# Sample attention with the queries in the partitions: keys and values stream through TensorE, later sums come from a backward scan

## What is computed

```python
def stick_breaking_block(q, k, v, q_pos, k_pos):
    z = jnp.einsum('bthd,bshd->bhts', q, k) * (SB_HEAD_DIM ** -0.5)
    mask = k_pos[None, :] < q_pos[:, None]
    log_fail = jnp.where(mask, jax.nn.log_sigmoid(-z), 0.0)
    after = lax.cumsum(log_fail, axis=3, reverse=True) - log_fail
    a = jnp.where(mask, jnp.exp(jax.nn.log_sigmoid(z) + after), 0.0)
    return jnp.einsum('bhts,bshd->bthd', a, v)
```

## Time and profile before

| | us |
|---|---|
| median of 3 runs | 1241.44 (1239.06 to 1242.43) |
| profiled execution, its time | 1239.74 |
| span of its trace | 1237.9 |
| PE busy | 1185.4 (96% of the span) |
| DVE busy | 743.7 (60%) |
| ACT busy | 461.7 (37%) |
| POOL busy | 293.5 (24%) |
| TensorE clock granted, mean | 0.964 |

### The profile page before, as it was taken

The page is one execution under the profiler, slowest core; times in us unless marked ns, Lnnn a source line. Parts: engine busy times, 40 slices in busy tenths (PEclk is TensorE's granted clock), DMA queues, the critical chain, the costliest instruction groups (busy, mean ns, idle before and its releaser), DMA issues.

```text
span 1237.9 us, 17578 instructions
## 1 busy us (share of the span) xinstructions
PE 1185.4 (96%) x6684; PEld 1122.9 (91%) x6684; DVE 743.7 (60%) x1316; ACT 461.7 (37%) x901; POOL 293.5 (24%) x318
## 2 busy tenths in 40 slices
PE   3999999999999999999999999999999999999994
PEld 2899889999989999988999989899999999998993
DVE  7758955687966588886378885476442133243118
ACT  4356532155542145643034644234402322252221
POOL 2114412113422123423013342120020011111225
PEclk9999988999998899998899998899999999999997
DMA  6130120015031115021014103202310111111144
GB/s 225 35 124 35 35 103 23 32 37 160 18 102 35 37 37 160 18 83 54 20 55 139 39 18 120 75 20 79 124 52 34 52 35 51 35 44 42 35 170 153
DMA packets 41460, 84.92 MB, mean 69 GB/s; under 512 B 2080, under 2 KB 22176, under 8 KB 41248
## 3 DMA queue, kind: packets, MB, share of 16 engines
q1 hardware_dynamic: 40800, 81.43, 19.8%
q10 hardware_dynamic: 576, 2.36, 0.5%
HBM read 67.27 MB, written 16.52 MB: 68 GB/s over the span
## 4 chain that ended last, share of the span: by engine, by line
PE 86%; DVE 9%; issue 2%; ACT 2%; DMA 1%; POOL 1%; SPq 0%; DVEq 0%; POOLq 0%; ACTq 0%
PE bank L619 51%; PE bank L907 7%; PE bank L692 5%; PE bank L732 5%; PE bank L753 3%; PE bank L784 3%; PE bank L830 2%; PE bank L853 2%; PE bank L679 1%; PE bank L678 1%; DVE SPsL L1461 1%; DVE xw L1333 1%; DVE imaskL L1294 1%; POOL SUs L1680 1%; DVE xl L1566 1%
## 5 line engine op out<-in xcount | busy, mean ns | idle before, releaser
L619 PE MATMUL bank<-xl,wh 128*128 128x384 f32 x1344 | 466.2, 347 | 6.7 <-DVE xl L1329 6.7
L619 PE MATMUL bank<-xh,wh 128*128 128x384 f32 x1344 | 464.0, 345 | 6.7 <-ACT xh L1088 3.5
L619 PE MATMUL bank<-xh,wl 128*128 128x384 f32 x1344 | 463.0, 344 | 0.0
L619 PEld LDWEIGHTS bank<-xl,wh 128*128 128x128 f32 x1344 | 260.0, 193 | 14.4 <-DVE xl L1329 8.2
L619 PEld LDWEIGHTS bank<-xh,wh 128*128 128x128 f32 x1344 | 260.4, 194 | 13.0 <-issue 8.4
L619 PEld LDWEIGHTS bank<-xh,wl 128*128 128x128 f32 x1344 | 259.4, 193 | 7.1 <-issue 3.4
L1241 DVE CAST wh<-wr 128x1024 fp32r<-128x1024 f32 x64 | 44.1, 689 | 107.2 <-PE bank L619 107.1
L1694 POOL TENSOR_TENSOR imaskH<-i_nat,k 128x512 fp32r<-128x512 f32 (+1 forms) x36 | 52.1, 1450 | 230.7 <-PE bank L830 230.7
L1032 ACT ACTIVATE slot<-bank,ngate 128x384 f32<-128x384 f32 x48 | 27.7, 578 | 199.1 <-PE bank L619 196.7
L1243 DVE TENSOR_TENSOR wl<-wr,wh 128x1024 fp32r<-128x1024 f32 x64 | 99.1, 1549 | 2.2
L1706 POOL TENSOR_TENSOR slot<-slot,slot 128x384 f32<-128x384 f32 x24 | 31.3, 1303 | 240.6 <-DVE slot L1562 240.6
(11 more groups left out here) (200 smaller groups left out, 1894.5 us busy)
## 6 DMA issues: line engine op xcount, KB each, us to landing
wr<-wch SPq DMA_DIRECT2D x64, 512.0 KB, 3.6
KTc<-ckT SPq DMA_DIRECT2D x4, 2048.0 KB, 9.8
Vc<-cv SPq DMA_DIRECT2D x4, 2048.0 KB, 8.4
xw<-xT SPq DMA_DIRECT2D x6, 768.0 KB, 9.9
graw<-gated SPq DMA_DIRECT2D x8, 576.0 KB, 6.1
xres<-xT SPq DMA_DIRECT2D x1, 4608.0 KB, 15.6
yT<-yb SPq DMA_DIRECT2D x6, 576.0 KB, 3.0
okT<-kT ACTq DMA_DIRECT2D x4, 576.0 KB, 3.0
```

The costliest lines, as they stand in the source:

```text
L619: i = nc.tensor.matmul(CH[n % 2][:, 0:WIN], weights[:, k, :], rows[:, k, w * WIN:(w + 1) * WIN], start=(m == 0), stop=(m == 23))
```

## The change

The sample attention is turned round. The queries become the stationary weights, 32 of them (one stream: 2 heads, 16 tokens), and the 512 cached keys of the stream move: 8 matmuls of 512 columns, each written to 32 partitions of a bank, four streams to a bank. So a query has its scores in one partition, and the later sums are a running sum along the row: DVE scans each row backward over 640 columns (`SW`: 512 cached and 128 new keys) and subtracts the sum from the scores. The splits into high and low, POOL's tile sums and the 18 sum matmuls fall away. For the values the keys must be in the partitions again: PE turns the weights by 10 transposes, ACT copies them to SBUF (`As`), and 32 matmuls take 32 query columns as weights while 128 value columns move. The output has the queries in the partitions; DVE copies it to `Os`, and PE turns it by two transposes in step 3, after which DVE gates it, now in step 3 too. The mask of the new keys is turned once at the start of the kernel. `gg`, `em`, `EK` and `EQ` stand behind the copies of step 1 on ACT, and DVE has its part of the sample attention ahead of the centring of the decays. Steps, pieces and the order of everything else stay.

```diff
+SW = PAST + P
...
-        Es = place("Es", [P, 5, 256])
-        SPs = place("SPs", [P, 5, 256])
-        SUs = place("SUs", [P, 3, 256])
+        Es = place("Es", [P, 2, SW])
+        CUs = place("CUs", [P, 2, SW])
+        As = place("As", [P, 5, 256])
         EK = place("EK", [P, TOK])
         EQ = place("EQ", [P, TOK])
...
+        Os = place("Os", [P, 256])
...
             pe.wait_ge(s_c, 32)
+            for g in range(2):
+                i = nc.tensor.transpose(OB[:, P * g:P * g + P], smask[:, P * g:P * g + P], ident)
+            i.then_inc(s_mt, 1)
             x_square_sum(0)
...
-                        qall = qbd[:, :, :, :].rearrange("p i h t -> p (i h t)")
-                        nc.tensor.matmul(Z[2][:, 0:256], kTs[:, :], qall, start=True, stop=True).then_inc(s_zs, 1)
-                        for half in (1, 0):
-                            for j2 in range(2):
-                                for s in range(STREAMS):
-                                    o = 256 * j2 + 32 * s
-                                    i = nc.tensor.matmul(Z[half][:, o:o + 32], KT_[:, s, P * (2 * half + j2):P * (2 * half + j2 + 1)],
-                                                         qall[:, 32 * s:32 * s + 32], start=(j2 == 0 and s == 0), stop=True,
-                                                         skip_group_check=True)
+                        for g in range(2):
+                            own = qbd[:, 4 * g:4 * g + 4, :, :].rearrange("p i h t -> p (i h t)")
+                            i = nc.tensor.matmul(Z[2][:, P * g:P * g + P], own, kTs[:, :], start=True, stop=True)
+                        i.then_inc(s_zs, 1)
+                        for g in range(2):
+                            for r in range(4):
+                                q = qbd[:, 4 * g + r, :, :].rearrange("p h t -> p (h t)")
+                                i = nc.tensor.matmul(Z[g][32 * r:32 * r + 32, :], q, KT_[:, 4 * g + r, :], start=True, stop=True)
                             i.then_inc(s_zs, 1)
                     if m == 1:
...
-                        for j in (3, 2, 1, 0):
-                            bk = Z[j // 2][:, 256 * (j % 2):256 * (j % 2) + 256]
-                            if j == 2:
-                                pe.wait_ge(s_Shs, p + 1)
-                                pe.wait_ge(s_Sls, p + 1)
...
+                        for g in range(2):
+                            pe.wait_ge(s_asm, 2 * p + g + 1)
+                            for j in range(4):
+                                nc.tensor.transpose(Z[g][:, P * j:P * j + P], Es[:, g, P * j:P * j + P], ident)
+                            nc.tensor.transpose(Z[2][:, P * g:P * g + P], Es[:, g, PAST:SW], ident).then_inc(s_ast, 1)
                     if m == 2:
                         pe.wait_ge(s_gA, 2 * (p + 1))
-                        pe.wait_ge(s_asm, p + 1)
-                        nc.tensor.matmul(OB[:, 0:256], vs[:, :], Es[:, 4, :], start=True, stop=True)
+                        pe.wait_ge(s_ate, p + 1)
+                        for g in range(2):
+                            nc.tensor.matmul(OB[:, P * g:P * g + P], As[:, 4, P * g:P * g + P], vs[:, :], start=(g == 0), stop=True,
+                                             skip_group_check=True)
                         pe.wait_ge(s_kv[1], 16 * (p + 1))
-                        pe.wait_ge(s_as, 3 * (p + 1))
                         for j in (3, 2, 1, 0):
-                            for s in range(STREAMS):
-                                i = nc.tensor.matmul(OB[:, 32 * s:32 * s + 32], V_[:, s, j, :], Es[:, j, 32 * s:32 * s + 32],
-                                                     start=False, stop=True, skip_group_check=True)
+                            for n in range(STREAMS):
+                                g, r = divmod(n, 4)
+                                i = nc.tensor.matmul(OB[32 * r:32 * r + 32, P * g:P * g + P], As[:, j, 32 * n:32 * n + 32],
+                                                     V_[:, n, j, :], start=False, stop=True, skip_group_check=True)
                         i.then_inc(s_os, 1)
+                    if m == 3:
+                        pe.wait_ge(s_oso, p + 1)
+                        for g in range(2):
+                            i = nc.tensor.transpose(OB[:, 2 * P + P * g:2 * P + P * g + P], Os[:, P * g:P * g + P], ident)
+                        i.then_inc(s_ost, 1)
...
+                    if m == 1:
+                        for g in range(2):
+                            act.wait_ge(s_cs, 2 * p + g + 1)
+                            nc.scalar.activation(Es[:, g, :], CUs[:, g, :], ACT.Exp).then_inc(s_as, 1)
+                        for g in range(2):
+                            act.wait_ge(s_ast, 2 * p + g + 1)
+                            nc.scalar.activation(As[:, 0:4, P * g:P * g + P], Z[g][:, :].rearrange("s (j c) -> s j c", j=4), ACT.Copy)
+                        nc.scalar.activation(As[:, 4, :], Z[2][:, 0:256], ACT.Copy).then_inc(s_ate, 1)
 
                         act.wait_ge(s_ge, 2 * (p + 1))
                         nc.scalar.activation(gg[:, :], be[:, :], ACT.Exp).then_inc(s_EX, 1)
...
+                        for g in range(2):
+                            e = Es[:, g, 0:PAST]
+                            dve.wait_ge(s_Ls, 3 * p + g + 2)
+                            V.scalar_tensor_tensor(e, e, 88.0, Z[g][:, :], ALU.min, ALU.max).then_inc(s_sps, 1)
+                            dve.wait_ge(s_sps, 3 * p + g + 2)
+                            dve.wait_ge(s_spm, p + 1)
+                            V.tensor_tensor_scan(CUs[:, g, ::-1], reset[:, 1:2].broadcast_to([P, SW]), Es[:, g, ::-1], 0.0,
+                                                 ALU.mult, ALU.add).then_inc(s_scu, 1)
+                            dve.wait_ge(s_scu, 2 * p + g + 1)
+                            V.tensor_tensor(CUs[:, g, 0:PAST], Z[g][:, :], CUs[:, g, 0:PAST], ALU.subtract)
+                            V.tensor_tensor(CUs[:, g, PAST:SW], Z[2][:, P * g:P * g + P], CUs[:, g, PAST:SW],
+                                            ALU.subtract).then_inc(s_cs, 1)
                         dve.wait_ge(s_scan, NT * (p + 1))
...
-                        V.tensor_copy(SPsH[:, :, :], SPs[:, :, :]).then_inc(s_sphs, 1)
...
-                        V.tensor_tensor(SPsL[:, :, :], SPs[:, :, :], SPsH[:, :, :].bitcast(F32), ALU.subtract).then_inc(s_spls, 1)
-                        V.tensor_copy(SUsH[:, :, :], SUs[:, :, :]).then_inc(s_Shs, 1)
...
-                        V.tensor_tensor(SUsL[:, :, :], SUs[:, :, :], SUsH[:, :, :].bitcast(F32), ALU.subtract).then_inc(s_Sls, 1)
...
-                        dve.wait_ge(s_as, 3 * p + 1)
-                        V.tensor_tensor(Es[:, 4, :], Es[:, 4, :], smask, ALU.mult).then_inc(s_asm, 1)
+                        for g in range(2):
+                            dve.wait_ge(s_as, 2 * p + g + 1)
+                            V.scalar_tensor_tensor(Es[:, g, PAST:SW], Es[:, g, PAST:SW], BIG, smask[:, P * g:P * g + P],
+                                                   ALU.min, ALU.mult).then_inc(s_asm, 1)
...
                         dve.wait_ge(s_os, p + 1)
+                        V.tensor_copy(Os[:, :], OB[:, 0:256]).then_inc(s_oso, 1)
...
-                            G.tensor_tensor(SUs[:, q, :], last, SPs[:, j, :], ALU.add).then_inc(s_Ss, 1)
```

More of the change, by code:

```diff
@@ L282, in build @@
         place = over(bt_o)
-        Es = place("Es", [P, 5, 256])
-        SPs = place("SPs", [P, 5, 256])
-        SUs = place("SUs", [P, 3, 256])
+        Es = place("Es", [P, 2, SW])
+        CUs = place("CUs", [P, 2, SW])
+        As = place("As", [P, 5, 256])
         EK = place("EK", [P, TOK])
         EQ = place("EQ", [P, TOK])
-        SPsH = place("SPsH", [P, 5, 256], F32R)
-        SUsH = place("SUsH", [P, 3, 256], F32R)
-        place = over(bt_o + 4 * 5 * 256)
-        SPsL = place("SPsL", [P, 5, 256], F32R)
-        SUsL = place("SUsL", [P, 3, 256], F32R)
+        Os = place("Os", [P, 256])
         place = over(kt_o)
@@ L410, in build @@
         s_asm = sem("sample_weights_masked")
+        s_ast = sem("sample_weights_turned")
+        s_ate = sem("sample_weights_turned_in_sbuf")
+        s_oso = sem("sample_out_in_sbuf")
+        s_ost = sem("sample_out_turned")
         s_os = sem("sample_values_added")
@@ L761, in _ @@
-                        nc.tensor.matmul(Z[2][:, 0:256], negtri_r[:, :], SPsH[:, 4, :], start=False, stop=True,
-                                         skip_group_check=True)
-                        nc.tensor.matmul(Z[2][:, 0:256], negtri_r[:, :], SPsL[:, 4, :], start=False, stop=True,
-                                         skip_group_check=True).then_inc(s_cs, 1)
-                        for j in (3, 2, 1, 0):
-                            bk = Z[j // 2][:, 256 * (j % 2):256 * (j % 2) + 256]
-                            if j == 2:
-                                pe.wait_ge(s_Shs, p + 1)
-                                pe.wait_ge(s_Sls, p + 1)
```

(32 more changed lines are left out.)

43 lines of the change are left out of this document (7 added, 36 removed).

## The result

| | before | with the change |
|---|---|---|
| median | 1240.88 (4 runs) | 1189.02 (1187.53 to 1189.71, 4 runs) |
| span of the profiled execution | 1237.9 | 1185.7 |
| ratio of the times | | 0.9581, interval 0.9567 to 0.9595 |

What follows compares the result with a forecast made beforehand. PE, busy 96% of the span, bounds the kernel. A stretch falls from 45.9 to 36.6 us; less 0.85 for clock, 8.45 is won, 34 in four: 1239.7 to 1206. Range of 8 in 10: 1188 to 1232.

Steps and rivals of the forecast that it cites:

- The scores and values on PE: Per stretch, cached scores 6.9 us where the old took 10.06; values 7.5 where the old took 0.4 and 8.98.
- own sign of being wrong: Wrong if the clock is low for 17 us of a stretch again, or the stretch is not near 37 us.
- the range of the mechanism itself: The forecast as summed, without its rivals: 1198 to 1220 us, chance 0.37.
- one after the other with loads hidden: PE's 32-column records run in sequence, weight loads costing nothing: 0.43 us per 512-column record, 0.11 per 128-column one.
- rival of side-by-side tiles: A stream's second record waits for its first, other tiles overlap: scores 3.9, values 3.6 us, total 1199; chance 0.25.
- perfectly fourfold case: Within the side-by-side rival, four column tiles overlapping fully, without loss of clock: 1185 us.
- DVE's chain: DVE's work up to the mask PE waits for: ends 16.6 us into the stretch, PE waits 2.4; scan 1.4.
- main claim: Streams of 512 and 128 columns keep PE's clock up: 8.5 us of the 9.3 gained per stretch.
- The fall behind the new wait: PE's clock falling after its 2.4 us wait for the mask: priced at 0.85 us a stretch.
- What should have been late next: Decay factors and their products end by 27 us, PE asks for them at 36: cover of 9 us.
- Exposed weight loads: Rival: 32-column matmuls wait for their own loads, 0.46 us per value record, 0.78 per score record; 1305 us, chance 0.13.
- The fallen clock: Rival: PE's clock falls because only 32 of 128 array columns work: 42.7 us a stretch, 1227; chance 0.20.

Runs made afterwards that it cites:

- both orders undone: The changed kernel with score matmuls ordered so two neighbours share a column tile, and value matmuls eight of one tile, then eight of the next: 1204.6 us.
- one tile at a time: The changed kernel with only the value matmuls reordered, all eight of one column tile, then all eight of the next: 1203.9 us.
- mask early: The changed kernel with DVE's two masks moved right behind the backward scans, ahead of the centring and the weight split: 1171.0 us.
- decay scans late: The changed kernel with DVE's sample chain and masks first, then the decay scans, centring and split: 1158.1 us, the fastest of all.
- pieces forward: The changed kernel with 9, 2 and 2 projection pieces in steps 0, 1 and 2 instead of 5, 4 and 4: 1173.6 us.

## Why the prediction was right, and where it was off

**What bounds, and where.** Right. PE set the time, and 50.6 of the span's 52.2 us came out of the four stretches.

**The scores and values on PE.** The direction was right, the size was not: this is the step that failed. By the forecast's own sign of being wrong it failed too: the stretch should have been near 37 us and is 33.4 in the mean. That 1189.0 lies inside the range is owed to the lower end, which had been drawn out to 1188 for a rival; the range of the mechanism itself, 1198 to 1220, missed it. So as far as the mechanism goes the hit is luck. And two errors partly cancel: the quick records gave more than forecast, the clock took back more. The forecast took "one after the other with loads hidden". Loads are hidden, but the records are not one after the other: 1.9 and 2.0 us instead of 6.9 and 7.0. Of the rival of side-by-side tiles, priced at 3.9 and 3.6, one assumption was wrong as well, that the second record of a stream blocks the next stream's first; TensorE passes it by. With both orders undone the kernel takes 1204.6, and the forecast for one-after-the-other was 1206. The agreement is better than the sums deserve, since in that kernel the scores stay quick and cost nothing either way, being ahead of a wait. The quick values alone are worth the 15 to 16 us that separate these kernels from the change, most of the 17 us by which the forecast was off. The perfectly fourfold case, which the prediction puts at 1185, comes to 31.4 us a stretch and 1182 by its own terms (16.6 + 1.2 + 5.5 + 2.2 + 5.5 + 0.35); the measured stretches are 31.4 as well when what the clock costs is taken off.

**DVE's chain.** Right almost term by term: the scan of 640 columns takes 1.49 us (1.4 from the row of 128 columns), and the transposes start at 16.5 us (16.6). The Trainium skill's page "DVE: opcode table, instruction layouts, handler registers and perf-mode slots" (Feedback) has this scan at half throughput; the trace agrees: from 128 to 640 columns it costs 2.1 ns a column, a plain operation 1.05. The wait was forecast as 2.4 and is 6.9, only because PE arrives at 9.6 and not at 14.2.

**The clock.** The forecast's main claim was that streams of 512 and of 128 columns keep the clock up. They do, even with one tile at a time. The fall behind the new wait was foreseen but priced too low, 0.85 us a pass; it costs 1.4 to 2.8 and happens in every pass. That the wait is 6.9 us long and not 2.4 explains only a part of this: with a wait of 2.8 us (mask early) it still happens in every pass and costs 1.4 to 1.7, and with 0.1 (decay scans late) it is gone. But pieces forward has waits of 1.6 and 2.7 us at the same place and no fall, so the length of the wait alone doesn't decide; what does wasn't isolated.

The split of the gain was off as well. The forecast had 8.5 of its 9.3 us a stretch from the clock and 0.8 from less work. Before, PE worked 68.3 us of the four stretches at the lower level, with the change 15.7. By half of each, the clock gave 26 of the 50.6 us; the other 24 are PE's shorter part less the longer waits. This is an estimate from the windows; no run separates the two.

**What should have been late next.** Nothing was, as forecast: the factors and their products end at 201.4 (28.2 us into the stretch; I had estimated 27), and PE has no wait at L800. The estimate was too short: DVE's L1472 takes 3.6 us instead of the 1.2 of the same line before (L1471), where POOL had nothing to do. The timelines of DVE and of POOL:

```profile
196.82 3.58 DVE L1472 TENSOR_TENSOR lf<-kb,gg 128x1024 f32<-128x1024 f32 x1
```

```profile
195.56 3.76 POOL L1676 TENSOR_TENSOR hq<-hq,EQ 128x1152 f32<-128x1152 f32 x1 [19.95 <-ACT EQ L1153]
```

L1472 ends at 200.40, 1.08 us behind the end of POOL's multiplication (199.32). That cost nothing here. In the fastest version DVE works nearly without a gap from these products to the row for which PE waits 0.9 us a pass, so it is likely the cause there; no run tests it.

**The rivals.** Exposed weight loads: refuted, since value records with 32 weight columns start every 0.109 us inside one tile, with a load of 0.11 us for each. The page "TensorE: Matmul & The Clock Gate" of the Trainium skill (Part 3) ties hidden loads to different row groups, or to a second weight buffer (Part 2); these matmuls all use all rows, so by Part 3 their loads would show, while Part 2 leaves a way for them to hide. The measurement decides: they hide. The fallen clock: refuted for these streams. Side by side: right, and fully fourfold. The page "TensorEngine Tiling (Array Packing)" of the Trainium skill (Key Properties) says that tiles work in parallel; the trace agrees with 1.9 us for 6.9 us of records.

## What to carry to other kernels

Matmuls with 32 output partitions cost a quarter when four of them, for the four partition groups, stand next to each other in the program; the same ones in blocks of eight by group cost three times as much. When such an edit makes the bound engine quick, count again who it waits for: here 6.9 us a pass went into a wait for another engine, and 31 us came from changing the order of that engine, not from less work. Put what the bound engine waits for first in its neighbour's queue, and everything that is wanted later behind it.

## What the runs showed of the hardware that was not expected

- Column tiles are passed by: with two matmuls (four records) of a tile next to each other, all four tiles still work at once (1.94 us for 16 records of 512 columns). With 16 records of a tile in a row they don't (5.96 us for 64 records of 128 columns, against 1.95). In the orders tried, the records of another tile start as soon as no tile ahead of them has more than three records still to start.
- The clock stays at its upper level while, but for short overlaps, only 32 of the array's 128 columns work without a gap for 5.9 us; it fell under matmuls of 128 weight columns and 32 moving ones.
- A product of 1024 columns on DVE takes 1.2 us alone. When an instruction of GpSimd is under way as it begins, it isn't slowed evenly but held: it ends 1.08 us behind the end of GpSimd's instruction, at 3.6 us (L1472) and at 1.4 to 1.7 (L1481). L1470, which begins 0.13 us ahead of GpSimd's, takes 1.36 us for 1152 columns, as it does alone, and the copy out of PSUM (L1479) takes 0.42 beside it.
